# Expert loop of a decoder-layer kernel: gather from three bfloat16 parts, gate columns finished first, two steps moved behind the gather

## What is computed

```python
def _expert(xb, e, w_gu, b_gu, w_dn, b_dn):
    gu = xb @ w_gu[e] + b_gu[e]
    g = jnp.minimum(gu[..., :D_EXPERT], SWIGLU_LIMIT)
    u = jnp.clip(gu[..., D_EXPERT:], -SWIGLU_LIMIT, SWIGLU_LIMIT)
    act = g * jax.nn.sigmoid(SWIGLU_ALPHA * g) * (u + 1.0)
    return act @ w_dn[e] + b_dn[e]
```

## Time and profile before

| | us |
|---|---|
| median of 3 runs | 1512.44 |
| lowest and highest run | 1510.73, 1513.79 |
| the profiled execution, its own time | 1507.18 |
| span of the profiled execution | 1505.4 |
| PE busy | 1426.2 (95% of the span) |
| DVE busy | 628.0 (42%) |
| ACT busy | 316.0 (21%) |
| HBM read over the span | 495.45 MB |

### The profile page before, as it was taken

One profiled execution on the slowest core, in us unless ns is written; L12 is line 12 of the kernel. 1 busy time (PEld: TensorE's weight loads), 2 busy tenths in 40 slices (PEclk: granted clock), 3 DMA queues, 4 the chain that ended last, 5 costly groups with the idle time before them and its releaser, 6 DMA issues. The chain is left out here.

```text
span 1505.4 us, 21718 instructions
## 1 busy us (share of the span) xinstructions
PE 1426.2 (95%) x8380; PEld 654.1 (43%) x8380; DVE 628.0 (42%) x1567; ACT 316.0 (21%) x590; POOL 85.6 (6%) x126
## 2 busy tenths in 40 slices
PE   4998899998899889999999999999999999999997
PEld 2456477777777443333333333333333333333332
DVE  2264334467774634543342333234233323423334
ACT  3013132256551111111111111111111111111110
POOL 1300000222202100000000000000000000000001
PEclk9999899999999979999999999999999999999999
DMA  9875734354324759999999999999999999999992
GB/s 341 250 284 199 277 149 147 128 185 142 141 113 159 291 192 414 424 427 427 426 428 428 428 428 427 428 427 428 428 427 428 427 428 428 427 428 427 428 428 91
DMA packets 65475, 501.73 MB, mean 333 GB/s; under 512 B 6432, under 2 KB 12500, under 8 KB 40583
## 3 DMA queue, kind: packets, MB, share of 16 engines
q1 hardware_dynamic: 55056, 463.07, 74.4%
q0 software_dynamic: 10368, 37.97, 7.4%
HBM read 495.45 MB, written 9.15 MB: 335 GB/s over the span
## 5 line engine op out<-in xcount | busy, mean ns | idle before, releaser
L1139 PE MATMUL bank_v<-arena 128*64 128x512 f32 (+13 forms) x4916 | 816.7, 468 | 30.3 <-DMA arena<-in_w_ada 11.8
L1139 PEld LDWEIGHTS bank_v<-arena 128*64 128x64 f32 (+7 forms) x4916 | 334.8, 137 | 485.0 <-issue 391.9
L1139 PE MATMUL bank_s<-arena 128*64 128x512 f32 (+3 forms) x1940 | 471.8, 555 | 5.0 <-DMA arena<-in_w_in 4.1
L1139 PEld LDWEIGHTS bank_s<-arena 128*64 128x64 f32 (+3 forms) x1940 | 176.4, 149 | 238.2 <-issue 204.3
L930 DVE TENSOR_SCALAR arena<-bank_v 128x512 f32<-128x512 f32 x32 | 22.1, 691 | 404.5 <-PE bank_v L1139 404.5
L950 DVE TENSOR_TENSOR arena<-bank_v,arena 128x512 f32<-128x512 f32 x128 | 82.4, 686 | 143.7 <-PE bank_v L1139 143.7
L1033 ACT ACTIVATE arena<-arena 128x512 f32<-128x512 f32 x32 | 20.2, 630 | 426.0 <-DVE arena L930 426.0
L1143 PEld LDWEIGHTS bank_s<-const_tables,arena 128*128 128x128 f32 (+3 forms) x605 | 73.5, 169 | 76.0 <-issue 37.7
L1143 PE MATMUL bank_s<-const_tables,arena 128*128 128x128 f32 (+3 forms) x605 | 96.3, 290 | 10.3 <-issue 3.0
L1641 DVE TENSOR_TENSOR arena<-bank_v,arena 128x288 f32<-128x288 f32 (+10 forms) x128 | 49.5, 387 | 92.5 <-PE bank_v L1139 64.8
L1039 ACT ACTIVATE arena<-bank_s 128x512 f32<-128x512 f32 x32 | 19.1, 598 | 312.6 <-PE bank_s L1139 312.6
(11 more groups left out here) (121 smaller groups left out, 622.8 us busy)
## 6 DMA issues: line engine op xcount, KB each, us to landing
arena<-in_w_gu SPq DMA_DIRECT2D x128, 2048.0 KB, 13.3
arena<-in_w_dn SPq DMA_DIRECT2D x64, 2048.0 KB, 11.0
arena<-in_w_ada SPq DMA_DIRECT2D x12, 2048.0 KB, 11.7
arena<-in_w_in SPq DMA_DIRECT2D x10, 2048.0 KB, 13.4
arena<-in_state_win_kv POOLq DMA_DIRECT2D x8, 512.0 KB, 7.0
arena<-in_w_out SPq DMA_DIRECT2D x2, 2048.0 KB, 19.4
out_win_sample<-in_state_win_kv POOLq DMA_DIRECT2D x1, 4064.0 KB, 27.4
x_rows<-in_x_prompt POOLq DMA_DIRECT2D x4, 512.0 KB, 8.7
```

The lines of the kernel that those rows point to most:

```text
L1139: return pe.matmul(out, l, r, start=first, stop=last)
```

## The change

Four edits, all in the expert loop and in what prepares it.

**Three-part gather.** `h2` is split before the loop into three bfloat16 parts: high = bf16(h2), middle = bf16(h2 - high), and low = bf16(h2 - high - middle); their sum gives the float32 value to its last bits or nearly. ACT makes seven copies with conversion (signals `high_parts`, `middle_parts`), DVE six subtractions (`rest_ready`, `parts_ready`). The first and second tile have three parts each (`first_parts`, `second_parts`); the 32 sample rows put their parts under each other in 96 partitions (`sample_parts`), for which the slot numbers of these rows are copied to two further partition groups. The gather in the loop is 2 tiles x 3 parts + 1 = 7 pairs of bfloat16 multiplications in place of 3 pairs in float32. The gather for block 0 (`first_gather`) stays in float32.

**Gate first.** In chunk 3 the gate columns of both row groups come ahead of the up columns, with a new signal `gate_filled` between. DVE clamps the gate columns then, ACT takes the sigmoid, DVE multiplies the two (`sgb`), and after `gu_filled` only two DVE steps stand before `act_ready`: the clamp of up and (u + 1) times `sgb`.

**Down bias and the samples' combine behind the gather.** Both now stand between `gather` and the transposes; token tiles are combined in the order 2, 0, 1 in place of 0, 1, 2.

The diff, cut to its core:

```diff
+        ohb = take(3, CAP, dt=BF16)
...
+                pe.wait_ge(sem("parts_ready"), 3)
+                for i, parts in enumerate((first_parts, second_parts)):
+                    for k in range(3):
+                        for half in range(2):
+                            mm(beside(5, half), ohb[:, i, :], parts[:, k, half * 512:(half + 1) * 512], (i, k) == (0, 0), False)
+                for half in range(2):
+                    last = mm(beside(5, half), ohb[0:96, 2, :], sample_parts[0:96, half * 512:(half + 1) * 512], False, True)
...
-                    for t in range(2):
-                        for q in range(2):
-                            for c in range(2):
+                    for t, q in ((0, 0), (0, 1), (1, 0), (1, 1)) if k < 3 else ((0, 0), (1, 0), (0, 1), (1, 1)):
...
+                        if (k, t, q) == (3, 1, 0):
+                            last.then_inc(sem("gate_filled"), 1)
...
-            v(spread_rows(0), "spread_ready")
+            v(spread_rows(oh, 0), "spread_ready")
+            for p0 in (32, 64):
+                copy(slot_of_tok[p0:p0 + 32, 2, 0:NEXP], slot_of_tok[0:32, 2, 0:NEXP])
...
-            ve.wait_ge(sem("rows_filled"), 1)
-            v(spread_rows(1), "spread_ready")
+            v(spread_rows(ohb, 1), "spread_ready")
+            for i, (o, n) in enumerate(TILES):
+                hi = (first_parts[:, 0, :], second_parts[:, 0, :], sample_parts)[i]
+                ve.wait_ge(sem("high_parts"), i + 1)
+                tt(rests[i][0:n, :], h2[0:n, i, :], hi[0:n, :], sub, "rest_ready")
+            for i, (o, n) in enumerate(TILES):
+                ve.wait_ge(sem("middle_parts"), i + 1)
+                if i < 2:
+                    parts = (first_parts, second_parts)[i]
+                    tt(parts[:, 2, :], rests[i], parts[:, 1, :], sub, "parts_ready")
+                else:
+                    tt(sample_parts[64:96, :], rests[i][0:n, :], sample_mid[0:n, :], sub, "parts_ready")
...
+            se.wait_ge(sem("h2_rows"), 6)
+            for i, (o, n) in enumerate(TILES):
+                hi = (first_parts[:, 0, :], second_parts[:, 0, :], sample_parts)[i]
+                act(hi[0:n, :], h2[0:n, i, :], ACT.Copy, "high_parts")
+            for i, (o, n) in enumerate(TILES):
+                se.wait_ge(sem("rest_ready"), i + 1)
+                if i == 2:
+                    act(sample_mid[0:n, :], rests[i][0:n, :], ACT.Copy)
+                mid = (first_parts[:, 1, :], second_parts[:, 1, :], sample_parts[32:64, :])[i]
+                act(mid, rests[i][0:n, :], ACT.Copy, "middle_parts")
```

More of the change, by code:

```diff
@@ L545, in program @@
         bsel_dn = take(CAP, dt=BF16)
+        ohb = take(3, CAP, dt=BF16)
         assert at[0] <= ARENA, at[0]
+        at[0] = gT.offset
+        first_parts = take(3, D, dt=BF16)
+        assert at[0] <= gT.offset + 8 * NTOK
+        at[0] = scale2.offset + D
+        second_parts = take(3, D, dt=BF16)
+        sample_parts = take(D, dt=BF16)
+        assert at[0] <= shift2.offset + D
+        rests = [squares, arena[:, gbuf.offset:gbuf.offset + D], x[:, 2, :]]
+        sample_mid = ub.bitcast(BF16)
         cb = arena[:, scale2.offset:scale2.offset + D].rearrange("p (a b) -> p a b", a=2)
@@ L642, in gather @@
                         last = mm(beside(5, half), oh[0:n, i, :], h2[0:n, i, half * 512:(half + 1) * 512], i == 0, i == 2)
+                last.then_inc(sem("rows_filled"), 1)
+            def gather(count):
+                pe.wait_ge(sem("spread_ready"), count)
+                pe.wait_ge(sem("parts_ready"), 3)
[5 more added lines that the diff above has]
+                    last = mm(beside(5, half), ohb[0:96, 2, :], sample_parts[0:96, half * 512:(half + 1) * 512], False, True)
                 last.then_inc(sem("rows_filled"), 1)
@@ L673, in pe_block @@
                     w = W[k].rearrange("p (t n) -> p t n", t=2)
-                    for t in range(2):
-                        for q in range(2):
-                            for c in range(2):
-                                last = mm(beside(q, c), xT[:, 2 * k + t, :], w[:, t, q * D + c * 512:q * D + (c + 1) * 512], False, k == 3 and t == 1)
+                    for t, q in ((0, 0), (0, 1), (1, 0), (1, 1)) if k < 3 else ((0, 0), (1, 0), (0, 1), (1, 1)):
+                        for c in range(2):
+                            last = mm(beside(q, c), xT[:, 2 * k + t, :], w[:, t, q * D + c * 512:q * D + (c + 1) * 512], False, k == 3 and t == 1)
+                        if (k, t, q) == (3, 1, 0):
+                            last.then_inc(sem("gate_filled"), 1)
                     last.then_inc(sem("gu_filled"), 1)
@@ L692, in pe_block @@
                     mm(beside(4, half), bsel_dn[0:96, :], bias3[0:96, b0:b0 + 512], True, False)
+                pe.wait_ge(sem("spread_turned"), e + 1)
+                pe.wait_ge(sem("sum_drained"), 3 * e + 1)
+                pe.sem_inc(sem("sum_seen"), 1)
+                combine(2, 2).then_inc(sem("sum_filled"), 1)
+                pe.wait_ge(sem("act_ready"), e + 1)
+                turn(6, ub, 4).then_inc(sem("act_turning"), 1)
+                pe.wait_ge(sem("rows_copied"), e + 2)
+                turn(7, xr, 2).then_inc(sem("rows_turning"), 1)
                 pe.wait_ge(sem("act_turned"), e + 1)
@@ L713, in pe_late @@
             pe.wait_ge(sem("bias_placed"), 16 * 9)
-            gather(1)
+            first_gather()
             b = fill(pe, "v", "count")
```

49 lines of the change are left out of this document (22 added, 27 removed).

## The result

| | before | after |
|---|---|---|
| median, us | 1512.53 (8 runs) | 1502.12 (8 runs) |
| lowest and highest | 1509.03, 1517.01 | 1495.55, 1506.64 |
| profiled execution, its own time | 1507.18 | 1497.62 |
| span | 1505.4 | 1495.8 |

The ratio of the runs is 0.993, 95% interval 0.9906 to 0.9954. The change makes the kernel faster, by 0.5 to 0.9%.

A forecast was written before the change was run, and what follows sets the result against it. PE was taken to set the pace, with the weight stream taking over once its reserve was gone. Gains of 8.8 + 1.2 + 0.3 = 10.3 us gave 1502.1 us, range 1498.5 to 1507.5.

The forecast's parts named there:

- The gather: Gather in each block: seven bfloat16 pairs (1.6 us) replace three float32 pairs (2.57 us), saving 0.95 us a block.
- Gate first: Before each block's first transpose: PE's wait of about 0.3 us for DVE goes, leaving 0.4 us of cover.
- The moved steps: Down bias and combine behind the gather: same PE cost, new 0.15 us wait for ACT's copy before chunk 4.
- Ahead of the loop: Added copies and subtractions before the loop: low parts done about 565.1 us, hidden with 2 us to block 0's gather.
- PE's period: PE's own time per block in the loop falls by 1.2 us to 28.15, bounds 0.9 to 1.35.
- The reserve: Lead of chunk 3's landing over PE's need: 11.4 us in block 3, gone after some nine blocks, then 1.3 us waits.
- The sum: Whole loop: 8.8 us from the sooner last gather, 1.2 in the last block, 0.3 at the start, together 10.3.
- The median: Median of the runs: 1512.44 us before, 5.3 above the profiled execution, falls with the same gain to 1502.1.
- A faster stream: Weight stream could exceed 427.6 GB/s, so PE stays the bound at 28.15: gain 38.6, 1473.8 us; 4 in 100.
- A slower stream: Undisturbed runs have a slower stream, reserve already used up: 1510.9 us, or 1506 if half so; 12 in 100.
- No shortening of PE's turn: Gather takes 5.5 us, period 32; or milder, new waits eat the gain, time stays 1512; 4 in 100.
- The clock: Chunk 3 from about block 12: PE's waits halve its clock, +42 over the forecast, 1544 us; 5 in 100.

The follow-up runs named there:

- gate_only: The kernel before with only the gate columns of chunk 3 first and DVE's new order, float32 gather kept; median 1508.3 us, ratio to before 0.9967.
- pad4: The changed kernel with 4 further useless bfloat16 pairs on PE ahead of each gather in the loop; median 1499.1 us.
- after_half5: The changed kernel with only half of down chunk 5 reloaded for experts 1 to 31; 1467.7 us, ratio to before 0.9724.
- before_half5: The kernel before with only half of down chunk 5 reloaded for experts 1 to 31; 1512.4 us, ratio to before 1.0008.
- both splits: The changed kernel with chunk 3's transfer split into gate and up columns: 1504.1 us; with five useless multiplications before the loop added: 1500.7 us.
- gather_only: The kernel before with only the three-part bfloat16 gather and its preparation; median 1512.8 us, ratio to before 1.0021.

## Why the prediction was right, point by point

**The bound.** Right: PE set the pace, the queue did not run dry after the first two blocks, and the reserve was nearly all there was to gain. The stream's last landings (1465.3 and 1475.1) stayed where they were.

**The gather.** Eight bfloat16 pairs, gather and down bias, take 1470.63 - 1468.80 = 1.83 us, 0.23 each as taken from the earlier trace rows. The saving of 0.95 us was sized too small even so. The float32 gather does not take 2.57 us but 2.82, as gate_only shows, and the seven new pairs alone take 1.52: the part is worth 1.3 us. The sum does not suffer, since it runs from the gather's start to the first down product, both read from the trace; what the gather has more, the wait for DVE has less, 0.19 us and not 0.3.

**Gate first.** This step was right in its sum and wrong in its reason. It took the 0.3 us ahead of the first transpose for a wait for DVE that would go. gate_only shows that nothing goes while the float32 gather stands, since the second set of transposes then waits for ACT's copy of the gathered rows, and the whole ends at the same point. In the full change both chains are shorter, and the first transpose starts at 2.40 us (forecast 2.43).

**The moved steps.** First down product at 3.83 us after the gather's start (forecast 3.85), with the forecast wait for ACT: 6.6 us in 32 blocks, 0.2 each (0.15).

**Ahead of the loop.** Right: the low parts are done at 566.28 us, 7.6 us after the first refill (forecast 7.8), and the gather of block 0 starts at 568.61, 9.9 us after it, as before. It waits for nothing.

```profile
565.06 1.22 DVE L1689 TENSOR_TENSOR arena<-x_rows,arena 32x1024 bf16<-32x1024 f32 x1
```

**PE's period.** 27.99 us, not 28.15. The saving is 1.35 us a block, at the upper bound. The missing 0.1 us is in chunk 5: its products now follow each other without a combine among them and take 1482.07 - 1478.48 = 3.59 us, against twice 1020.34 - 1018.48 = 1.86, or 3.72 in the block of the earlier trace rows.

**The reserve.** It was to be 11.4 us in block 3 and gone nine blocks later, with waits of 1.3 us from about block 12, in 20 blocks. The waits came some three blocks earlier, in the last 23 blocks, and cost more: a little over 1.2 us in the view and 1.43 us by the spacing. The 11.4 us are the reserve of the kernel before in that block. The changed kernel had spent 3.0 us of it by then (17.5 us to landing against 14.5), and spent 1.43 us in each further block, not 1.28. The time does not depend on this, because the stream sets the end either way.

**The sum.** Forecast 8.8 + 1.2 + 0.3 = 10.3 us. From the first refill to the end, free of what comes ahead of it, the change is worth 948.1 - 937.1 = 11.0 us. Of these, 8.8 are the sooner start of the last gather in the span, and 1.4 the shorter refilling (908.0 to 906.6 us from first refill to last chunk 3), where 0.3 of a range 0 to 1.7 was taken. The tail from the last gather to the end gives 27.0 against 27.8 us, 0.8, where 1.2 was taken. The block itself gained 1.3; the last combine at the end, at half clock, took 3.42 us where it had taken 1.99. The first two 30 us of the loop, which moved 416 GB/s, still lose in the first one, 412, and no longer in the second, 428. The 1.4 us were given back by a later start of the loop in this execution, 558.67 against 557.28 us.

**The median.** 1502.12 us against 1502.1 owes something to luck: the first eight runs had a low mean clock, 0.975, and two terms of the sum were off by 1.1 and 0.4 us with opposite signs. All 19 runs have a median of 1500.2, and at equal clock the gain is 11.7 us, 0.8%.

**The rivals.** A faster stream: refuted by pad4 and after_half5. A slower stream: refuted. The 5.3 us between profile and median fit the clock: the profiled execution of before had 0.980, where the median of its kind is 1506.7 us. They lie ahead of the loop as far as the profiles show: before_half5, the same loop for PE, has its first refill 2.7 us earlier, at 554.54, and the same loop and tail, 948.1. Single runs without a profile cannot be looked into. No shortening of PE's turn: refuted for the whole, though true of each part alone. The clock: it stayed at 1.00 beside waits of 1.2 to 1.3 us per block in five profiles (the changed kernel twice, both splits, gather_only from the sixth block on). But gather_only shows that the mechanism is real: waits of 1.51 and 1.83 us were each followed by a fall, at 1.65 to 1.8 us per fall. The passage of the Trainium skill that was weighed there ("TensorE: Matmul & The Clock Gate", "HAM oscillation — how this bites in real kernels") tells of waits of some 3 to 5 us for each transfer. No run here has waits of that length in the loop, so the passage says nothing of waits of 1.3 us, and the prediction read more into it than it says. A fall at every wait did not come.

## What to carry to other kernels

When two resources both read as busy, compare their periods, not their shares: the spacing of issues against the spacing of landings told that only some 10 us of a possible 38 were to be had, and a growing time from issue to landing is the reserve being spent. A saving in one of two chains that end together is worth nothing until the other is shortened too, so parts of a change that show nothing alone may still be worth keeping together. And where times scatter with the clock, compare at equal clock, or from an event inside the program.

## What the runs showed that was not expected

- Waits of 1.51 and 1.83 us on PE were each followed by some 3.5 us of half clock that cost 1.65 to 1.8 us. Waits of 1.48 and 1.49 us in the next three blocks were not, and waits of 1.3 us in every block were not, over 790 us.
- The waits as listed were 0.2 us shorter than what they cost by the spacing of the blocks (1.2 against 1.43 us), for the most part because a wait is counted from the modelled end of the multiplication before it.
- Splitting one 2 MiB transfer of six in two of 1 MiB, with pieces of 4 KB in place of 16 KB, took the stream from 428 to 425 GB/s.
- The scatter of whole runs, 16 us, follows the mean granted clock: from 0.974 to 0.980 the median falls by 8.2 us.
